# Where SBUF buffers begin: moving every large buffer of a fused two-block model to a multiple of 128 bytes

## The reference, cut to what matters

```python
def first_block(x, c, ...):
    for l in range(2):                       # hybrid_layer
        shift, scale, gate = split(c @ w_ada + b_ada)
        h = (x * (1 + scale) + shift) @ w_in          # 3938 columns
        o = concat(dsa_mixer(...), fox_mixer(...), nsa_mixer(...))   # three attentions
        y = (o * silu(h["gate"])) @ w_out
        x = layer_norm(ALPHA * x + (1 + gate) * y)
    return x

def second_block(x, ...):
    for layer in range(2):
        m = hybrid_mixer(x, ...)             # 31-tap convolution, gated delta rule
        x = layer_norm(A * x + m)
        f = swiglu(x) if layer == 0 else moe_swiglu(x)   # dense, then 8 experts, top 2
        x = layer_norm(A * x + f)
    return x
```

## The kernel before

| buffers | before | after |
|---|---|---|
| `ring`, `ring_r`, `uT`, `uT_r`, `const` | 0 | 0 (not moved) |
| `const2`, `x`, `rows`, `vecs`, `lng`, `lnb`, `router_w` | 96 | 0 |
| first block: `perow`, `pe_sb`, `w2`, `p_sb`, `pT` | 0 | 0 |
| first block: `raw_*`, `rot_*`, `rope_t2`, `ksS`, `kwS`, `blk`, `otmp`, `stat` | 96 | 0 |
| first block: `gate1p`, `dv`, `fq`, `fk`, `fv`, `vsw`, `ff`, `ident_r`, `causal_r`, `ff_r` | 32 | 0 |
| first block: `vblk`, `sg`, `mix`, `isc`, `isw`, `select_r` | 64 | 0 |
| mixers: `wba`, `cvrow`, `cvec`, `cacc`, `sig`, `qkvpad` | 0 | 0 |
| mixers: `hpad`, `ong`, `qkv`, `sq`, `sz`, `ktok`, `kT`, `vb`, `kdec`, `decay`, `attnT`, `lev`, `S1` | 32 | 0 |
| dense part: `ff_hi`, `u_lo`, `h_hi`, `h_lo`, `hs` | 0 | 0 |
| experts: `more_raw`, `his`, `xe_*`, `he_*`, `ye_*`, `total`, `pick` | 0 | 0 |
| experts: `pickT` | 32 | 0 |

## Time and profile before

### The profile page before, as it was taken

How to read it: one execution, slowest core, us unless ns; L and a number is a source line. 1 busy time by engine, 2 the same in 40 slices (tenths; PEclk the granted TensorE clock), 3 DMA queues, 4 the chain that set the end, 5 groups by cost and what they waited for, 6 DMA issues and landing times.

```text
span 2154.8 us, 28044 instructions
## 1 busy us (share of the span) xinstructions
PE 2088.3 (97%) x10596; PEld 1665.9 (77%) x10596; DVE 1510.5 (70%) x1837; ACT 1006.0 (47%) x1082; POOL 50.9 (2%) x56
## 2 busy tenths in 40 slices
PE   7999999999998999999889999999999999999996
PEld 4786677756876799888747888888888888888885
DVE  4565434554597445438848888898888889888887
ACT  1121312122133334313236777777777777677674
POOL 0000000000011000000200000000000000000000
PEclk9998999999999999999988999999999999999999
DMA  9844043611621265452127999999999999999990
GB/s 356 279 140 159 30 146 99 226 43 38 217 79 40 92 202 196 172 183 81 44 107 291 395 355 368 347 355 372 330 374 337 367 346 355 376 327 375 333 368 20
DMA packets 238710, 502.18 MB, mean 233 GB/s; under 512 B 11275, under 2 KB 53027, under 8 KB 238627
## 3 DMA queue, kind: packets, MB, share of 16 engines
q1 hardware_dynamic: 238626, 501.03, 65.0%
HBM read 499.96 MB, written 1.05 MB: 233 GB/s over the span
## 4 chain that ended last, share of the span: by engine, by line
PE 89%; DVE 7%; ACT 2%; issue 1%; DMA 0%; SPq 0%; DVEq 0%; ACTq 0%
PE bank L1506 12%; PE bank L1489 9%; PE bank L1491 9%; PE bank L1490 9%; PE bank L757 6%; PE bank L1196 6%; PE bank L989 3%; PE bank L1064 3%; PE bank L765 3%; PE bank L1166 3%; PE bank L1433 3%; PE bank L1172 2%; PE bank L1404 2%; PE bank L1403 2%; PE bank L1402 2%; PE bank L1368 2%
## 5 line engine op out<-in xcount | busy, mean ns | idle before, releaser
L2650 DVE TENSOR_TENSOR ring_r<-ring,his 128x2048 fp32r<-128x2048 f32 x240 | 548.7, 2290 | 77.9 <-ACT his L1619 77.2
L1619 ACT ACTIVATE his<-ring 128x2048 fp32r<-128x2048 f32 x240 | 460.2, 1918 | 127.5 <-PE bank L1491 74.7
L1489 PE MATMUL bank<-his,xe_hi 128*128 128x512 f32 x896 | 354.1, 395 | 0.2 <-DVE ring_r L2650 0.2
L1491 PE MATMUL bank<-his,xe_lo 128*128 128x512 f32 x896 | 349.5, 390 | 0.0
L1490 PE MATMUL bank<-ring_r,xe_hi 128*128 128x512 f32 x704 | 274.2, 389 | 0.0
L2650 DVE TENSOR_TENSOR more_raw_r<-more_raw,his 128x2048 fp32r<-128x2048 f32 x96 | 219.7, 2290 | 27.5 <-ACT his L1619 27.4
L1619 ACT ACTIVATE his<-more_raw 128x2048 fp32r<-128x2048 f32 x96 | 184.2, 1919 | 54.6 <-PE bank L1506 29.1
L1489 PEld LDWEIGHTS bank<-his,xe_hi 128*128 128x128 f32 x896 | 168.2, 188 | 37.0 <-DVE ring_r L2650 3.3
L1491 PEld LDWEIGHTS bank<-his,xe_lo 128*128 128x128 f32 x896 | 168.2, 188 | 35.9
L1490 PEld LDWEIGHTS bank<-ring_r,xe_hi 128*128 128x128 f32 x704 | 132.3, 188 | 26.7
L1196 PE MATMUL bank<-uT,ring 128*128 128x256 f32 (+1 forms) x768 | 149.1, 356 | 0.0
(11 more groups left out here) (439 smaller groups left out, 3093.4 us busy)
## 6 DMA issues: line engine op xcount, KB each, us to landing
ring<-in_moe_w_gate_dram SPq DMA_DIRECT2D x96, 1024.0 KB, 5.2
ring<-in_moe_w_up_dram SPq DMA_DIRECT2D x80, 1024.0 KB, 5.3
ring<-in_moe_w_down_dram SPq DMA_DIRECT2D x64, 1024.0 KB, 4.9
more_raw<-in_moe_w_down_dram SPq DMA_DIRECT2D x48, 1024.0 KB, 5.0
ring<-in_w_in_dram SPq DMA_DIRECT2D x16, 2048.0 KB, 11.4
more_raw<-in_moe_w_up_dram SPq DMA_DIRECT2D x32, 1024.0 KB, 5.2
ring<-in_w_ada_dram SPq DMA_DIRECT2D x12, 2048.0 KB, 10.8
ring<-in_w_out_dram SPq DMA_DIRECT2D x8, 2048.0 KB, 9.6
```

The costliest lines, as they stand in the source:

```text
L1489: mm(bank[b][:, :], xe_hi[:, k, :], hi[:, kk, :], start=(k == 0), stop=False)
L1491: last = mm(bank[b][:, :], xe_lo[:, k, :], hi[:, kk, :], start=False, stop=(k == KD - 1))
L1619: return go(out, in_, ACT.Copy, scale=scale)
L2650: tt(piece_lo(s), piece_raw(s), piece_hi(s).bitcast(fp32), ALU.subtract).then_inc(S("lo_ready"), 1)
```

## The change

`sb` looks at the size of each buffer it makes. If that is not a multiple of 128 bytes, and the name is neither on a list of small tables (`LOOSE`) nor begins with `sm_`, a filler buffer follows that brings the next start to a multiple of 128. The small tables are made at the end of their stage in place of the middle, and `items` moves from the shared part to the end of the expert stage. No instruction is added, removed or put elsewhere; only the addresses in them differ.

```diff
+LINE = 128
+LOOSE = ("lnst", "lnmv", "logits", "best", "gates", "hot", "chosen", "places", "comb", "long", "item_f", "items", "cstat", "cmv", "osq", "eps_col", "b_f", "adac", "iw", "sgate", "chrep", "kcT", "m8", "ch", "cmp_s", "pairs_r")
...
         def sb(name, shape, dtype=fp32):
-            return place[0].enter_context(nc.sbuf_tensor(name, shape, dtype))
+            made = place[0].enter_context(nc.sbuf_tensor(name, shape, dtype))
+            over = math.prod(shape[1:]) * 4 % LINE
+            if over and not name.startswith("sm_") and name not in LOOSE:
+                place[0].enter_context(nc.sbuf_tensor(f"{name}_fill", [P, (LINE - over) // 32 * 8 or 8], fp32))
+            return made
...
         router_w = sb("router_w", [P, KD, NE])
-        items = sb("items", [P, 4 * NE + 1], mybir.dt.int32)
...
-        b_f = sb("b_f", [FOX_HEADS, DEPTH])
         gate1p = sb("gate1p", [P, D])
-        adac = sb("adac", [P, 16])
...
         stat = sb("stat", [P, 4, 4, 8])
+        b_f = sb("b_f", [FOX_HEADS, DEPTH])
+        adac = sb("adac", [P, 16])
+        iw = sb("iw", [P, NT, IDX_HEADS])
+        sgate = sb("sgate", [P, NT, 18])
+        chrep = sb("chrep", [HD, NSA_GROUPS, NSA_HPG, NCMP])
+        kcT = sb("kcT", [P, NSA_GROUPS, NCMP])
+        m8 = sb("m8", [P, NT, 8])
+        ch = sb("ch", [HD, 3, 2, NSA_GROUPS * NCMP])
+        cmp_s = sb("cmp_s", [P, NT, NSA_HEADS, NCMP])
+        pairs_r = sb("pairs_r", [32 + FOX_HEADS, FOX_HEADS], fp32r)
         first.close()
...
         item_f = sb("item_f", [P, 4 * NE + 1])
+        items = sb("items", [P, 4 * NE + 1], mybir.dt.int32)
         fourth.close()
```

More of the change, by code:

```diff
@@ L449, in build @@
         ksS, kwS = sb("ksS", [P, T]), sb("kwS", [P, T])
-        iw = sb("iw", [P, NT, IDX_HEADS])
         dv = sb("dv", [P, NT, HD])
@@ L457, in build @@
         ff_r = sb("ff_r", [32 + FOX_HEADS, T], fp32r)
-        pairs_r = sb("pairs_r", [32 + FOX_HEADS, FOX_HEADS], fp32r)
-        sgate = sb("sgate", [P, NT, 18])
         blk = sb("blk", [P, 2, CMP_LEN // 2, NSA_GROUPS, NCMP])
-        ch = sb("ch", [HD, 3, 2, NSA_GROUPS * NCMP])
-        chrep = sb("chrep", [HD, NSA_GROUPS, NSA_HPG, NCMP])
-        kcT = sb("kcT", [P, NSA_GROUPS, NCMP])
         vblk = sb("vblk", [NHC, NSA_HEADS, HD])
@@ L473, in build @@
         select_r = sb("select_r", [P, NT, T], fp32r)
-        m8 = sb("m8", [P, NT, 8])
         p_sb, pT = sb("p_sb", [P, 2, 512]), sb("pT", [P, 2, 512])
         relu, rope_t1 = p_sb, sg[:, 0, :].rearrange("p (a t) -> p a t", a=2)
-        cmp_s = sb("cmp_s", [P, NT, NSA_HEADS, NCMP])
         otmp = sb("otmp", [P, NSA_HEADS * HD])
         stat = sb("stat", [P, 4, 4, 8])
+        b_f = sb("b_f", [FOX_HEADS, DEPTH])
[8 more added lines that the diff above has]
+        pairs_r = sb("pairs_r", [32 + FOX_HEADS, FOX_HEADS], fp32r)
         first.close()
```

## The result

The changed kernel takes 2160.67 us (median, 2155.81 to 2165.36) against 2153.84 us for the kernel before, measured side by side: ratio 1.003, 95% interval [1.0023, 1.0037]. So it is slower, by 6.8 us in the medians. That is inside the forecast range and within the 0.5% called "same", but the forecast said 2152 and a term near 0, and the interval tells the difference from nothing. A later measurement gave 1.0022 [1.001, 1.0034].

What follows compares the result with a forecast made beforehand. The prediction took TensorE as the bound, busy 2088.3 of 2154.8 us. Only 0.2 us came off, with all other terms 0, giving 2154.6 and 2157.2 with the surrounding 2.6; as a median 2152 us, range 2142 to 2161.

Steps and rivals of the forecast that it cites:

- same: Whole kernel: time within about 0.5%, 10.8 us, of no change; chance 0.80.
- Which instructions are touched: Heavy rows' buffers keep their place within 128 bytes, leaving at most 4558 matmul records in attention and mixers.
- the bound of 4.6 us: TensorE in attention and mixers: at most 4558 matmuls times 1 ns, 4.6 us; taken as 0.
- the 0.2 for `pickT`: 64 matmuls of 512 columns at L1476 and L1477 go from 393 to 390 ns, saving 0.2 us.
- VectorE, ScalarE and GpSimd at 0: Durations on these three engines do not change with the new starts; each term 0 us.
- whichever taps they are: VectorE's convolution: groups of eight taps take 3.25 us at every start, so no start is dearer.
- The rival "GpSimd": Mixers: 24 GpSimd products gain up to 17.7 us, giving 2134.9; chance 0.12, shared with other gains over 0.5%.
- DMA at 0: Transfers lie under TensorE's work except the last store of half of `x`, 2.6 us, unchanged; term 0.
- the slower rival of the weight stream: Expert stage: transfers into `more_raw` 43% slower make TensorE wait, 2177.2 us; chance 0.08, shared with other such losses.
- Slower, equal starts get in each other's way: Attention and mixers: engines on equally placed buffers lose 0.35%, 3.3 us, giving 2155.9; counted within the 0.80.
- Faster, engines pay for odd starts: Matmuls and VectorE instructions in the moved stages gain 6.0 us, giving 2146.6; counted within the 0.80.
- The other sign: Mixers: TensorE's idle time changing by more than 10 us would also prove the prediction wrong.

Runs made afterwards that it cites:

- experiment 1: Changed kernel with 128 bytes of filler moving only the experts' buffers back to their old starts: 2152.22 us, ratio 0.9995 to the kernel before.
- experiment 2: Kernel before with 128 bytes of filler, moving only the experts' buffers to multiples of 256 bytes: 2166.93 us, ratio 1.0063.
- experiment 5: Changed kernel with fillers so that the ring buffers too, like all in the expert stage, start at multiples of 256 bytes: 2150.83 us, ratio 0.9985.
- experiment 3: Changed kernel with 128 bytes of filler ahead of `xe_hi`, so stationary operands move and `his` and `more_raw` stay: 2163.48 us, ratio 1.005.
- experiment 4: The map: TensorE alone, float32r matmuls of 512 columns, both starts stepped by 32 bytes over 512; experts' order 226.7 to 227.2 ns alike, up to 233.4 otherwise.
- experiment 6: TensorE alone, maps of 64 start pairs for other float32r widths and plain float32; plain float32 429.2 ns at 512 columns in every cell.
- experiment 9: The kernel of experiment 1 measured again: 2152.91 us, ratio 0.9984 to the kernel before.
- experiment 12: TensorE alone, the same placements repeated in another order, some after a pause; 512 columns: 226.65 ns all alike, 229.0 to 233.4 for the changed kernel's.

## Why the prediction was wrong

**The step that failed is "Which instructions are touched".** It said that the buffers of the heavy rows "do not change their place within 128 bytes", and left the expert stage out of every term. The starts had been reduced modulo 128, a number taken from the change and from no row. The map shows that for float32r matmuls of 512 columns the period is 256 bytes. By that measure the experts' buffers did move against the ring, and the stage with the most matmuls and no gap on TensorE lost 10.4 us. Experiments 1, 2 and 5 show the cause in the kernel (moved back, moved alone, moved all together), 3 and 4 the form of it: the start of the moving operand against that of the stationary one. That the measured median still lies inside the range, 0.3 us below its upper end, is luck: no term of the sum and no bound of the range priced this.

**The form of the terms was too narrow.** I asked of each row whether its operands are aligned. What counts is whether they are alike, and a row in which both stand at 32 can't be told from one in which both stand at 0. Those rows are also plain float32 of 128 columns, where the map of experiment 6 is flat, so they could say nothing about float32r of 512. It isn't a matter of each operand, so it could not be found by going through the buffers one at a time.

**TensorE, the bound of 4.6 us and the 0.2 for `pickT`.** The bound was not broken where it was laid, in attention and mixers, but it didn't hold for the kernel, since the dense and expert stages were outside it. The dense stage changed by -2.13 and +0.74 us. The row with `pickT` was said to fall from 393 to 390 ns; it rose to 396:

```profile
L1183 PE MATMUL bank<-const,qkv 128*128 128x128 f32 x32 | 4.1, 272 | 0.0
L1183 PE MATMUL bank<-const,qkvpad 128*128 128x128 f32 x32 | 4.1, 272 | 0.0
...
L1483 PE MATMUL bank<-ye_lo,pickT 128*128 128x512 f32 x32 | 12.7, 396 | 0.0
```

The 3 ns that the prediction priced, and these 3 as well, are within what this row does by itself: it reads 393 and 394 ns in two profiles of the old layout (before and experiment 2), 396 and 394 in two of the changed kernel, and 394 and 398 in experiments 1 and 9, which are one and the same kernel. So no run shows the term of 0.2 us. Nor does the map ask for a change here: `pickT` and `ye_lo` stood at 160 and 128 modulo 256 before and stand at 128 and 0 after, unlike in both, and the map has some 233 ns for either. The `const` rows, plain float32 of 128 columns, stayed equal, as the flat map of that shape says.

**VectorE, ScalarE and GpSimd at 0** held. The taps shown take 3.25 us a group of eight, the copies 597 and 598 ns, and GpSimd's row fell by 17 ns, 24 times, 0.4 us:

```profile
565.61 3.25 DVE L2480 SCALAR_TENSOR_TENSOR cacc<-hpad,cvec,cacc 128x256 f32<-128x256 f32 x8
```
```profile
L2065 POOL TENSOR_TENSOR lev<-qkvpad,const 128x512 f32<-128x512 f32 x24 | 33.5, 1413 | 229.4 <-ACT qkvpad L1625 166.8 <-PE bank L1178 62.6
```

The rival "GpSimd" is out by this: of its 17.7 us, at most 0.4 were there, and a second profile of the changed kernel has 1426 ns for this row. The prediction also placed GpSimd in the mixers' chain, but the chain of the earlier trace rows has no share for it.

One reading of the taps was too quick. They do not take 3.25 us "whichever taps they are": in the profile before, 12 of the 240 took 1481 to 1502 ns in place of some 478, and each of the 12 began while a GpSimd product was running. The changed kernel has the same 12 taps at 1480 to 1493 ns, although `hpad` now starts elsewhere, so the place isn't what makes them slow and the term of 0 stands. That GpSimd is the cause fits but was not tested, and one tap that also began beside a GpSimd product, at 1043.90 us, took 474 ns. Two lines of the kernel before, with two such taps among the eight:

```profile
634.90 5.29 DVE L2474 SCALAR_TENSOR_TENSOR cacc<-hpad,cvec,cacc 128x256 f32<-128x256 f32 x8
...
635.16 2.76 POOL L2059 TENSOR_TENSOR lev<-qkvpad,const 128x512 f32<-128x512 f32 x2 [4.16 <-PE bank L1172]
```

**DMA at 0** held, and with it the slower rival of the weight stream is out: `more_raw` lands in 5.1 us, 0.1 less than before, and TensorE's matmuls waited for `more_raw_r` 0.5 us in all, before and after. The same rows answer the rule cited from the Trainium skill ("DMA: Bandwidth & Descriptors", section "How a descriptor splits into AXI transactions"): the 6% that it would give if it held for writes into SBUF are 0.3 us, and they don't show. The up pieces land in `more_raw` in 5.2 or 5.3 us where it is odd and in 5.1 where it is even, the down pieces in 4.9 or 5.0 in both. What makes the 0.1 us of the up pieces is open.

```profile
ring<-in_moe_w_up_dram SPq DMA_DIRECT2D x80, 1024.0 KB, 5.2
...
more_raw<-in_moe_w_up_dram SPq DMA_DIRECT2D x32, 1024.0 KB, 5.1
```

**The rivals.** "Slower, equal starts get in each other's way" came nearest of the rivals to the measured 2160.67, with 2155.9, but for a wrong reason: VectorE's product of 2048 stayed at 2290 ns, and for TensorE's 512 columns equal starts are the best there is. "Faster, engines pay for odd starts" asked the right engine about the wrong stages. The statement of what would make the prediction wrong was useful: "if a matmul row of unchanged shape moves by more than 2 ns". The rows of `ring_r` did, from 389 to 395. But 2 ns is too fine for some rows: `sq` with `lev` in the mixers went from 283 to 287 and was back at 283 in the second profile of the changed kernel. The other sign stayed away: TensorE idled 31.4 us in the two mixer windows after, against 31.5 before.

**What stays open.** Of the 5.2 us between the two profiles' spans, the experts explain more than the whole; -2.41 and -1.41 us fall in stages in which the old placement never ran against a moved one by itself. Two executions of the changed kernel differ by 5.8 us in the first of these (725.21 and 719.39), so that it is no effect of the change that could be claimed. The second appears in all profiles of the new layout (217.6 to 217.9 against 219.3 and 219.5) and was not taken apart. Why TensorE's pace depends on the two starts at all is not shown by any run, nor what sets its size, which for the changed kernel's placement went from 229.0 to 233.4 ns in experiment 12.

## What to carry to other kernels

Where TensorE runs without gaps on float32r matmuls of 512 columns, look at the starts of moving and stationary operands modulo 256 bytes and make them alike; a layout that is neat for each buffer by itself can part them, and then a stage loses 1%. Before a change of addresses is costed, take the period from a measurement and not from the change. When starts are compared, add up means: the median here said 20 ns for three steps where the stage paid 10. A map made on one engine is a price only if the cell repeats in another order: at 512 columns the alike cell did, and the unlike one stayed dearer by a varying amount; the fast cells of 256 columns did not.

## What the runs showed of the hardware

- Float32r matmuls of 512 columns follow each other in 226.6 to 229.6 ns when both operands begin at the same place modulo 256 bytes and in up to 234.3 when not, with a second dip (228.9 to 229.7) where the stationary operand starts 64 bytes lower than the moving one. In the order of `his`, `ring_r`, `his` with the ring 128 off, one placement took 229.0, 230.9 and 233.4 ns at different times of one run.
- Plain float32 matmuls did not depend on the starts (429.2, 215.8 and 111.7 ns for 512, 256 and 128 columns), and float32r ones of 128 columns didn't either (111.5 to 112.0). Float32r of 384 columns took 173.0 to 176.7, and 173.3 to 175.2 with equal starts.
- At 256 columns of float32r the sign is turned round: the dense gate-up takes 120.0 ns alike and 117.8 with the changed kernel's starts. Placements whose moving operands start 64 bytes higher were seen at 117.8 and at 113.3 ns with nothing changed but what ran before.
- VectorE's taps took some 478 ns each; 12 of 240, each begun while a GpSimd product was running, took 1481 to 1502 ns.
